# One block for the gates and the delta stage, and a first stage that transposes ahead, in a hybrid decoder layer on one core

## The reference

```python
def _layer(x, p, C, n, m, S, conv_buf, ...):
    h = _rmsnorm(x, g_mix)
    proj = h @ w_in
    (q_a, k_a, v_a, i_pre, f_pre, o_a, qkv_b, a_b, beta_b, z_b, gate_a, gate_b) = jnp.split(proj, ...)
    ha, C, n, m = _mlstm(q_a, k_a, v_a, i_pre + b_igate, f_pre + b_fgate, C, n, m)      # 4 heads
    ...
    cv, conv_buf = _causal_conv(qkv_b, conv_buf, conv_w)                                # 4 taps
    cv = silu(cv)
    q_b, k_b = _l2norm(cv[..., :1024]), _l2norm(cv[..., 1024:2048]);  v_b = cv[..., 2048:]
    g = -exp(a_log) * softplus(a_b + dt_bias)
    beta = sigmoid(beta_b)
    hb, S = _gated_delta(q_b, k_b, v_b, g, beta, S)                                     # 8 heads
    ...
def _gated_delta(...):        # per chunk of tokens
    gam = cumsum(g);  decay = exp(gam_i - gam_j) for i >= j
    a_mat = I + strict(kb k^T * decay)
    w_v, w_k = triangular_solve(a_mat, [v * beta, kb * exp(gam)])
    ...
```

## Time and profile before

| | |
|---|---|
| median of three runs | 2870.58 us |
| lowest, highest | 2865.84, 2871.01 us |
| the profiled execution, its span | 2863.52 us, 2861.8 us |
| first stage, gate stage, first turn of the head loop | 0 to 86, 86 to 141, 141 to 265 us |

### The profile page before, as it was taken

The page is one execution under the profiler, slowest core; times in us unless marked ns, Lnnn a source line. Parts: engine busy times, 40 slices in busy tenths (PEclk is TensorE's granted clock), DMA queues, the critical chain, the costliest instruction groups (busy, mean ns, idle before and its releaser), DMA issues.

```text
span 2861.8 us, 40512 instructions
## 1 busy us (share of the span) xinstructions
PE 2615.3 (91%) x16191; PEld 2539.6 (89%) x16191; DVE 1154.3 (40%) x1932; ACT 640.3 (22%) x1319; POOL 627.7 (22%) x322
## 2 busy tenths in 40 slices
PE   4379999999999699999589999999999999999997
PEld 3269999999998599999489999999999999999897
DVE  2445655665565124524331321653223133134534
ACT  3235544554454111111100000011001000010112
POOL 2232121212120111111032222442222212112421
PEclk7689999999999899999799999999999999999998
DMA  3121221221110215334521211211111111111211
GB/s 115 22 83 48 70 62 32 69 69 56 38 53 25 78 47 93 50 80 70 109 49 45 100 45 44 102 46 46 47 44 45 45 38 45 45 44 38 75 30 70
DMA packets 235322, 165.33 MB, mean 58 GB/s; under 512 B 23211, under 2 KB 222443, under 8 KB 235151
## 3 DMA queue, kind: packets, MB, share of 16 engines
q1 hardware_dynamic: 217414, 154.69, 19.5%
q10 hardware_dynamic: 17792, 8.95, 2.1%
HBM read 135.84 MB, written 27.76 MB: 57 GB/s over the span
## 4 chain that ended last, share of the span: by engine, by line
PE 25%; issue 19%; POOL 3%; DVE 2%; DMA 1%; ACT 0%; POOLq 0%; DVEq 0%; ACTq 0%
PE bank L227 22%; POOL t_w_lo L216 3%; PE bank L239 2%; PE bank L2408 1%; DVE t_rlo L2544 0%; DMA t_w_raw<-in_w_in_dram 0%; PE bank L2445 0%; DVE t_rhi L2541 0%; DVE hlo L2570 0%; DVE hhi L2567 0%; POOL t_rlo L2256 0%; DMA t_rraw<-HB 0%; POOL t_acc L2264 0%; DVE hraw L2714 0%; DVE t_x L2636 0%
## 5 line engine op out<-in xcount | busy, mean ns | idle before, releaser
L216 POOL TENSOR_TENSOR t_w_lo<-t_w_raw,t_w_hi 128x1024 fp32r<-128x1024 f32 x112 | 270.0, 2411 | 952.3 <-DVE t_w_hi L211 952.3
L227 PE MATMUL bank<-t_rhi,t_w_lo 128*128 128x384 f32 (+1 forms) x1248 | 410.4, 329 | 8.6 <-POOL t_w_lo L216 8.6
L227 PE MATMUL bank<-t_rhi,t_w_hi 128*128 128x384 f32 (+1 forms) x1248 | 409.9, 328 | 0.0
L227 PE MATMUL bank<-t_rlo,t_w_hi 128*128 128x384 f32 (+1 forms) x1248 | 409.8, 328 | 0.0
L227 PE MATMUL bank<-hhi,t_w_lo 128*128 128x384 f32 (+1 forms) x1224 | 399.0, 326 | 3.2 <-POOL t_w_lo L216 3.2
L227 PE MATMUL bank<-hhi,t_w_hi 128*128 128x384 f32 (+1 forms) x1224 | 399.2, 326 | 0.0
L227 PE MATMUL bank<-hlo,t_w_hi 128*128 128x384 f32 (+1 forms) x1224 | 398.9, 326 | 0.0
L227 PE MATMUL bank<-hhi,b_w_lo 128*128 128x384 f32 (+1 forms) x768 | 270.6, 352 | 10.0 <-POOL b_w_lo L216 10.0
L227 PE MATMUL bank<-hlo,b_w_hi 128*128 128x384 f32 (+1 forms) x768 | 252.6, 329 | 0.0
L227 PE MATMUL bank<-hhi,b_w_hi 128*128 128x384 f32 (+1 forms) x768 | 252.4, 329 | 0.0
L227 PEld LDWEIGHTS bank<-t_rhi,t_w_lo 128*128 128x128 f32 x1248 | 236.8, 190 | 9.3 <-POOL t_w_lo L216 9.1
(11 more groups left out here) (371 smaller groups left out, 4319.1 us busy)
## 6 DMA issues: line engine op xcount, KB each, us to landing
b_w_raw<-in_w_in_dram SPq DMA_DIRECT2D x32, 512.0 KB
t_w_raw<-in_w_up_dram SPq DMA_DIRECT2D x32, 512.0 KB, 3.8
t_w_raw<-in_w_down_dram SPq DMA_DIRECT2D x32, 512.0 KB, 3.8
a_w_raw<-in_w_in_dram SPq DMA_DIRECT2D x24, 512.0 KB
t_w_raw<-in_w_in_dram SPq DMA_DIRECT2D x16, 512.0 KB, 3.7
b_gam<-ROWS_B SPq DMA_DIRECT2D x8, 576.0 KB, 5.2
b_eg<-ROWS_B SPq DMA_DIRECT2D x8, 576.0 KB, 3.7
b_kb<-ROWS_B SPq DMA_DIRECT2D x8, 576.0 KB, 3.7
```

The lines of the kernel that those rows point to most:

```text
L216: pool.tensor_tensor(self.lo[j % 2][:, 0:kt, :], self.raw[j % self.rs][:, 0:kt, :], self.hi[j % 2][:, 0:kt, :], ALU.subtract).then_inc(sel ...
L227: ins = pe.matmul(out, a[:, k, :], b[:, k, :], start=(start and k == 0 and i == 0), stop=(stop and k == kt - 1 and i == 2))
```

## The change

The first stage. `sq` exists twice and `rb` three times; `hf` of groups 1 and 2 goes into the two `sq` buffers. DVE no longer waits for the small rows ahead of its first copy, but for the norm's gains ahead of chunk 6. PE runs its transposes up to chunk 4 before the first sums, up to 6 before the second and to the end before the third. ACT takes the casts to `hhi` from DVE, and DVE the subtraction of group 2 from POOL. DVE does all copies, then all products.

Gates and delta. `gates` becomes a set of pieces (`gate.loads`, `gate.product`, `gate.softplus`, ...) that `delta` calls inside its own block: the barrier between the two stages is gone. Head 0's turn is written out anew on every engine as `first_turn`, with the gate pieces between. PE multiplies the gate columns, then the K and Q slabs of head 0; then come K's norms, the V slab, the gate transposes, Q's norms, the first group of K of head 1, p1, the rest of K, the Z slab, and from there the old order. The gate product uses banks 6 and 7, as do K's norms (`KB0`) and the transposes; `FB` and `ZB` share the other six. The gate tiles lie over ZS, GAM, EG, KB, DT and others of `delta`, which are written only after `gate.done` or after the last gate column is copied. `TT` keeps 72 numbers of a chunk instead of 384. `WKM` and `QDM` are zeroed after `gate.done`.

```diff
-                sq = sb("sq", [P, KT, 384])
-                rb = sb("rb", [P, 384])
+                sq = [sb(f"sq{i}", [P, KT, 384]) for i in range(2)]
+                rb = [sb(f"rb{g}", [P, 384]) for g in range(NG)]
...
+                def hf_of(g):
+
+                    return (hf, sq[0], sq[1])[g][:, :, 0:GROUPS[g][1]]
...
-                        for g, (a, w) in enumerate(GROUPS):
+                        for g in range(2):
+                            a, w = GROUPS[g]
                             pool.wait_ge(s_hhi, g + 1)
-                            pool.tensor_tensor(hlo[:, :, a:a + w], hf[:, :, 0:w], hhi[:, :, a:a + w],
-                                               ALU.subtract).then_inc(s_hlo, 1)
...
+                            pool.tensor_tensor(hlo[:, :, a:a + w], hf_of(g), hhi[:, :, a:a + w], ALU.subtract).then_inc(s_hlo, 1)
...
+                            if c in (4, 6):
+                                sums(c // 2 - 2)
+                        sums(2)
...
+                        squares(2)
+                        logs(1)
+                        logs(2)
+                        exps(1)
+                        exps(2)
+                        for g in range(NG):
+                            high(g)
...
+                        for g in range(NG):
+                            scaled(g)
...
+                        dve.tensor_tensor(hlo[:, :, a:a + w], hf_of(2), hhi[:, :, a:a + w], ALU.subtract).then_inc(s_hlo, 1)
...
+                        src = psum[6 + c % 2][:, 0:3 * P].rearrange("p (i q r) -> p i q r", i=3, r=32)
+                        act.activation(TT[:, c], src[:, :, 1:4, 0:8], ACT.Copy).then_inc(s_tc, 1)
...
+            FB = Banks(psum[0:3], dense(K_), sem, "b_first")
+            KB0 = Banks(psum[6:8], normed(K_), sem, "b_first_norm")
+            ZB = Banks(psum[3:6] + psum[0:3], early, sem, "b_zero")
...
+                        gate.loads(sp)
                         slab(0, K_, 0, 0)
...
+                        slab(0, Q_, 1, 0)
+                        gate.moves(sp)
+                        slab(0, V_, 2, 0)
+                        gate.stores(sp)
+                        for i in (0, 2, 1):
                             row(0, i)
-                        slab(0, Q_, 1, 0)
+                        slab(0, K_, 3, 1)
+                        sp.wait_ge(gate.done, 1)
                         samples(0)
...
+                        WS.split_lo(pool, 0, 3)
+                        pool.wait_ge(gate.done, 1)
+                        pool.memset(WKM[:], 0.0).then_inc(s_zero, 1)
+                        pool.memset(QDM[:], 0.0).then_inc(s_zero, 1)
+                        unit_lower(0)
...
+                        def first_turn():
+                            gate.product(pe)
+                            for g in range(NG):
+                                whole(-1, K_, g, 0, 0)
+                            for g in range(NG):
+                                whole(0, Q_, g, 0, 1)
+                            pe.wait_ge(s_mask, MASKS)
+                            gate.taken(pe)
+                            norm(-2, 0, K_)
...
+                            for g in range(NG):
+                                whole(0, V_, g, 0, 2)
...
+                            gate.turned(pe)
+                            norm(0, 0, Q_)
+                            whole(0, K_, 0, 0, 3)
+                            wait(pe, kb, 0, 1)
+                            products(0, "p1", KN, KB)
...
+                        first_turn()
+                        for t in range(3):
+                            taken(pe, 0, ("wk", t))
...
+                            gate.exponents(dve)
...
                         unit(0, K_, KN)
+                        for i in range(1, W):
+                            conv(0, Q_, i)
+                        split(0, 3, 0, Q_)
+                        dve.wait_ge(s_mask, MASKS)
+                        gate.tables(dve)
+                        exponents(0)
                         scaled_k(0)
-                        turn(0, False, True)
+                        lower(0)
+                        for i in range(1, W):
+                            conv(0, V_, i)
...
+                        gathered(0)
+                        spread(0)
+                        split(0, 4, 0, V_)
...
         stage(prologue)
-        stage(gates)
         stage(delta)
```

More of the change, by code:

```diff
@@ L422, in _, with copy, squares @@
                     def _(act):
-                        act.wait_ge(s_const, 11)
-                        for g in turned(act, 0, lambda o, i: act.activation(o, i, ACT.Copy)):
+                        def copy(o, i):
+                            return act.activation(o, i, ACT.Copy)
+                        def squares(g):
                             a, w = GROUPS[g]
@@ new lines, in exps, with high @@
+                        def exps(g):
+                            w = GROUPS[g][1]
+                            act.wait_ge(s_ln, g + 1)
+                            act.activation(rb[g][:, 0:w], rb[g][:, 0:w], ACT.Exp, scale=-0.5).then_inc(s_rs, 1)
+                        def high(g):
+                            a, w = GROUPS[g]
+                            act.wait_ge(s_hf, KT * (g + 1))
+                            act.activation(hhi[:, :, a:a + w], hf_of(g), ACT.Copy).then_inc(s_hhi, 1)
+                        act.wait_ge(s_const, 11)
@@ new lines, in _ @@
+                        for c in range(3):
+                            turned(act, 0, c, copy)
+                        squares(0)
+                        for c in range(3, 6):
+                            turned(act, 0, c, copy)
+                        squares(1)
+                        logs(0)
+                        exps(0)
+                        for c in range(6, NCH):
+                            turned(act, 0, c, copy)
+                        squares(2)
+                        logs(1)
@@ L697, in delta @@
+            return gate
         def delta():
@@ L1243, in turn @@
                             first_tap(h, h, Q_)
[L1245 to L1247 removed]
+                            replicas(h)
                             if scan:
@@ L1315, in turn, with replicas @@
                                 evict(h, ("wk", t), WKT, scale=-1.0)
-                        halo(0, K_)
-                        for g in range(NG):
-                            copy_out(-1, K_, g)
-                        first_tap(-1, 0, K_)
-                        silu(0, K_, KN)
-                        squares(0, K_, KN)
-                        logs(-1, K_)
-                        exps(-1, K_)
-                        decays(0)
-                        turn(0, False, True)
+                        def replicas(h):
+                            for i, (a, w) in enumerate(((0, 512), (512, NCH * S8 * S8 - 512))):
+                                src = read(act, h, ("rep", i))
+                                release(act.activation(AR[:, a:a + w], src[:, 0:w], ACT.Copy), h, ("rep", i))
@@ L1572, in _ @@
                         wait(dve, half, 0, 1)
[L1573 to L1576 removed]
+                        gate.cumulate(dve)
                         for i in range(1, W):
```

669 lines of the change are left out of this document (384 added, 285 removed).

## The result

| | median us | lowest to highest | ratio to before, 95% interval |
|---|---|---|---|
| before | 2870.8 (4 runs) | 2865.8 to 2873.9 | |
| after | 2831.4 (4 runs) | 2824.7 to 2833.7 | 0.986 (0.984 to 0.988) |

The change gains 39.4 us; 33.9 was forecast (2837 against 2831). Measured again later, the changed kernel took 2832.0 beside 2867.6, a ratio of 0.988 (0.986 to 0.989).

What follows compares the result with a forecast made beforehand. Bound by TensorE's waits before the second head's turn: first stage 12.9 plus block 21.0 (21.7 less 0.7) gives 33.9; 2863.5 less 33.9 is 2829.6, with 7.1 carried over 2837. Range 2815 to 2858, own case 2827 to 2847.

Steps and rivals of the forecast that it cites:

- First stage, forecast 12.9: First stage: earlier copies, doubled square buffers and moved work end it at 72.0 instead of 84.9 us, 12.9 gained.
- a mis-sized hold: First stage: POOL's two subtractions and DVE's products exclude each other for whole instructions, POOL holding 6.7 us each time.
- V's cold restart: Head 0's V slab: after TensorE's stand it starts cold at +55.3, costing 2.7 us on top of 12.0.
- the rival of three slow slabs: V, head 1's K and Z slabs stay at low clock to their end: 22 us lost, 2859; chance 0.13.
- the slower one: Gate product and head 0's K and Q slabs also stay at 1.2 GHz: another 29 us, 2887; chance 0.04.
- V on the path, alone: Block: V slab queues behind K's norms, which wait for the first Ln; TensorE stands from +46.4, V starts +55.3.
- The alternation of POOL and VectorE: Head 0: POOL's six masked products and V's three convolution steps alternate, 6.2 + 4.2 us, to +105.8.
- the eviction wait: After the solver's level begins: PE waits for the last eviction before the loop, 0.7 us lost.
- No hold at all: DVE and POOL don't hold each other off: 23.0 in first stage, 4.2 more in block, 2822; chance 0.17.
- Slabs that don't run beside the gate chain: Block: K and Q slabs start only after the gate chain, so 24 us come back: 2861; chance 0.06.
- The table switches: Mixing gate chain and head 0 puts two more on the path, 1.28 us each; at the skill's 2.7, 2840.
- the 7 us: Whole kernel: three-run median 2870.6 lay 7.1 above the profiled 2863.5; carried over, 2829.6 became 2837.

Runs made afterwards that it cites:

- VectorE's own subtractions: Changed kernel with all three first-stage subtractions on VectorE, none on POOL: 2819.2 us, ratio 0.985.
- two kernels with one of two waits taken away: Changed kernel with a third bank for head 0's K norms (ratio 0.987), or with gate columns ahead of Q's SiLU on ACT (ratio 0.985).
- the one with both: Changed kernel with the third bank for K's norms and the gate columns ahead of Q's SiLU on ACT: 2817.5 us, ratio 0.984.
- the six products: Changed kernel with head 0's six masked products of unit_lower on VectorE instead of POOL, ahead of V's convolution: ratio 0.986.
- the new order: Changed kernel with head 0's turn reordered, every wait seen in its trace taken off the chain, and three subtractions on VectorE: 2798.5 us, ratio 0.976.
- the kernel with the slab ahead: Changed kernel with head 1's K slab issued directly behind V's slab, ahead of the gate stores and exponent rows: 2815.9 us, ratio 0.984.

## Why the prediction was right, step by step

**First stage, forecast 12.9, measured 17.2.** Two terms were too large. The sums took 5.43, 5.43 and 6.04 instead of 6.5, 6.5 and 5.6, so the products of groups 1 and 2 began at 44.05, not at 45.2; that 1.2 hangs on the clock of this one profile (43.6 to 47.3 in the other profiles with this stage). The rest, 3.1, is a mis-sized hold. I let two products of group 2 wait behind POOL's second subtraction, with their cast and the last subtraction behind them. In the trace all products were done at 58.4, since POOL began at 47.1 and VectorE had 3.8 us free between the two holds; the last cast ran on ACT beside the hold, and only the subtraction waited (60.86 to 65.0). The mechanism held: a 6.7 us hold of VectorE's products, then POOL's second subtraction at 7.36 instead of 6.7, since a product was running when it came. The Trainium skill (SBUF — State Buffer, "Who interferes with whom") has the rule that such a VectorE instruction with two SBUF inputs and a GpSimd instruction that reads SBUF exclude each other for a whole instruction, and the trace and the kernel without POOL's subtractions agree: 14.41 against 8.02.

**The block up to the columns.** Forecast and measured, from the block's start: product end 21.2 and 21.3; VectorE's gate run 37.0 and 37.4; end of the first Ln 54.1 and 55.2; V's start 55.3 and 56.0, its end 70.0 and 69.3; columns 74.5 and 73.6. Two errors cancel here. I hadn't counted that POOL's subtraction of the V slab stops a copy of eight elements on VectorE (111.11, 2.40 instead of 0.15), in the middle of the gate run. And V's cold restart cost 1.2, not 2.7: the slab took 13.25 us for 72 matmuls. A granted clock of 0.77 from 125 to 130 and 1.00 from 130 to 135 rules out a V slab that stays slow to its end; the K slab's matmuls are short (0.34) from 161.48 on, and Z took 14.1 us for its 72, so the rival of three slow slabs falls, and with it the slower one.

What the forecast had incomplete is the reason: it put V on the path, alone. ACT's chain through SiLU and squares ended at the same moment, so the bank that makes TensorE wait costs nothing by itself. The time was right, and someone who had acted on it would have gained 1.6 us at most.

**The slab, and the rest of the turn.** The slab landed at +83.3 (84.0 forecast), VectorE stood until then, and the masked products began at +93.6 (94.1). The alternation of POOL and VectorE ended at +104.5 (105.8): POOL's products took 2 us each while the convolution ran. The solver began at +131.2 (133.9); the Z slab's restart was 0.6 cheaper. From there to head 1 the changed kernel lost 2.2 us, not 0.7: 23.8 from the solver to the masked products against 21.6, 0.96 of it the eviction wait, 0.76 the first level's wait for VectorE; before, TensorE had neither. So 22.2 for the block where 21.0 was forecast, and 39.4 in all where the sum was 33.9.

**The rivals.** No hold at all (2822) fell with VectorE's own subtractions. Slabs that don't run beside the gate chain (2861): TensorE was busy for all of the 37.5 us from 76.5 to 114, through product, K and Q. The table switches took 1.28 each, as before. The Trainium skill (ScalarE: Activation LUTs, "Table sets") budgets 2.7 us; by that the gain would have been smaller than forecast, and it was larger. Carrying the 7 us between the profiled execution and the median over to the forecast was right, since they turned out to be run-to-run spread in a stage that stayed as it was.

## What to carry to other kernels

Before you mend a wait, look for the other chain that ends at the same place: by the landmark two kernels with one of two waits taken away gained 1.6 and -1.8 us, the one with both 9.9. A load whose issue stands behind a wait on its queue, while its buffer is long free, is the cheapest thing to look for (one moved line, 10 us). Where VectorE and GpSimd exclude each other, moving work to the engine that does it in half the time can shorten the stretch, even if that engine is the busier one: 5.5 us with the three subtractions, but only 0.7 with the six products, part of which had run beside VectorE.

## What the runs showed of the hardware that I had not expected

Small copies on VectorE wait for POOL too. The copy of 8 elements to `g_mprev` took 2.40 us beside POOL's subtraction (0.16 for the one just before it). The copy to `b_hg` took 2.01 us while POOL did nothing but two memsets, and 0.18 in the new order, which has the memsets elsewhere. So a memset, which reads nothing, holds off such a copy as well. In ten profiles the copy and the pair of memsets start together: in six the copy waits for both (2.01), in four, the kernel with the slab ahead among them, for the first alone (1.07). That the one waiting goes next, as the prediction has it, is therefore not a rule without exception, and a landmark behind this copy moves by 0.9 us for no reason of the kernel's.

POOL was slowed as well. Its `affine_select` over 64 columns took 0.29 us at 95.05, beside almost nothing on VectorE, and 0.67 to 0.83 in five cases from 97.1 on, beside VectorE's gate run; over 128 columns it took up to 2.46, where the kernel before has 0.29. Two rows show what it waited for:

```profile
98.77 2.42 DVE L698 TENSOR_TENSOR_SCAN g_cum<-g_reset,g_abs 128x1088 f32<-128x1088 f32 x1
98.84 2.45 POOL L1002 TENSOR_SCALAR_AFFINE_SELECT b_sm<-b_sm 128x128 f32<-128x128 f32 x1
```

POOL's instruction starts 0.07 us behind VectorE's scan and ends 0.1 us behind it. The five over 64 columns do the same with a copy or a `tensor_scalar` of VectorE that started just before them.

A TensorE that is early can lose its lead to the clock: 21 transposes that followed 8.6 us of standing took 4.54 us (granted clock 0.60 from 137 to 143), while 27 that came straight behind a slab took 4.02 at 1.00.
